# A routed-expert loop on one Trainium2 core: the down products moved one expert later, half of their weights split into two rounded parts, and five buffers for high parts instead of four

## The reference, cut to what matters

```python
def moe(hn, router_w, router_b, w_gu, b_gu, w_down, b_down):
    ...
    top_vals, top_idx = lax.top_k(logits, TOP_K)
    gates = jax.nn.softmax(top_vals, axis=-1)
    ...
    gu = lax.ragged_dot(xs, w_gu, group_sizes) + b_gu[sorted_e]
    gate = jnp.minimum(gu[:, ::2], SWIGLU_LIMIT)
    up = jnp.clip(gu[:, 1::2], -SWIGLU_LIMIT, SWIGLU_LIMIT)
    act = (up + 1.0) * (gate * jax.nn.sigmoid(SWIGLU_ALPHA * gate))
    y = lax.ragged_dot(act.astype(w_down.dtype), w_down, group_sizes) + b_down[sorted_e]
    y = y * gates.reshape(-1)[order][:, None].astype(y.dtype)
    out = jnp.zeros_like(xt).at[tok].add(y.astype(xt.dtype))
```

## Time and profile before

| | |
|---|---|
| three runs, median (range) | 3121.55 us (3121.18 to 3123.78) |
| span of the profiled execution | 3126.7 us |
| what lies around its span | no row gives it; span less median is 5.15 us |
| experts, from the start of the second to the end of the last | 422.60 to 1688.10 us, 31 experts |
| PE busy | 2762.4 us, 88% of the span |
| DVE, ACT, POOL busy | 56%, 37%, 9% |
| DMA, mean over the span | 203 GB/s |

### The profile page before, as it was taken

How to read it: one execution, slowest core, us unless ns; L and a number is a source line. 1 busy time by engine, 2 the same in 40 slices (tenths; PEclk the granted TensorE clock), 3 DMA queues, 4 the chain that set the end, 5 groups by cost and what they waited for, 6 DMA issues and landing times.

```text
span 3126.7 us, 32895 instructions
## 1 busy us (share of the span) xinstructions
PE 2762.4 (88%) x11604; PEld 2039.8 (65%) x11604; DVE 1756.8 (56%) x1942; ACT 1170.9 (37%) x1248; POOL 279.3 (9%) x336
## 2 busy tenths in 40 slices
PE   6987589999999999999996673498999989799997
PEld 4766456666666666666664343476888868588885
DVE  5764646666555555666664973546763354443333
ACT  4232345555555555555552130233222232232321
POOL 1230310000000000000002900000110000000000
PEclk9998699999999999999998785798999999999998
DMA  6742579999999999999996109333774333223432
GB/s 238 251 112 102 178 283 334 335 341 335 336 334 330 333 331 330 335 332 337 335 338 220 40 0 100 46 100 116 221 211 109 92 94 81 67 81 94 112 93 64
DMA packets 368731, 634.93 MB, mean 203 GB/s; under 512 B 45020, under 2 KB 238756, under 8 KB 368484
## 3 DMA queue, kind: packets, MB, share of 16 engines
q1 hardware_dynamic: 346244, 539.29, 54.0%
q0 software_dynamic: 17296, 76.03, 7.2%
q10 hardware_dynamic: 5136, 18.88, 1.5%
HBM read 610.10 MB, written 24.58 MB: 203 GB/s over the span
## 4 chain that ended last, share of the span: by engine, by line
PE 79%; DVE 10%; DMA 4%; ACT 2%; SPq 2%; POOL 1%; issue 1%; DVEq 0%; POOLq 0%; ACTq 0%
PE bank L1933 22%; PE bank L1949 15%; PE bank L2094 10%; PE bank L2095 10%; PE bank L2100 10%; PE bank L1922 2%; SPq L480 2%; PE bank L1911 1%; PE bank L1917 1%; PE bank L1760 1%; DMA ring<-k_dram 1%; PE bank L1795 1%; DVE work L1497 1%; PE bank L1796 1%; PE bank L1797 1%
## 5 line engine op out<-in xcount | busy, mean ns | idle before, releaser
L1415 DVE TENSOR_TENSOR gu_lo<-ring,gu_hi_ca 128x2048 fp32r<-128x2048 f32 x128 | 290.7, 2292 | 461.4 <-ACT gu_hi_ca L870 461.2
L1949 PE MATMUL bank<-ring,work 128*128 128x512 f32 x1024 | 458.9, 601 | 22.0 <-ACT work L882 22.0
L1949 PEld LDWEIGHTS bank<-ring,work 128*128 128x128 f32 x1024 | 190.2, 191 | 257.3 <-issue 227.7
L1933 PE MATMUL bank<-gu_lo,xs_hi 128*128 128x512 f32 x1024 | 316.1, 390 | 0.0
L1415 DVE TENSOR_TENSOR gu_lo<-ring,gu_hi_nat 128x2048 fp32r<-128x2048 f32 x128 | 290.7, 2291 | 28.8 <-ACT gu_hi_nat L870 28.3
L2094 PE MATMUL bank<-h_hi,fin_hi 128*128 128x512 f32 x704 | 277.7, 395 | 22.1 <-ACT h_hi L972 22.1
L2095 PE MATMUL bank<-h_hi,fin_lo 128*128 128x512 f32 x704 | 276.4, 393 | 0.0
L870 ACT ACTIVATE gu_hi_nat<-ring 128x2048 fp32r<-128x2048 f32 x128 | 241.9, 1920 | 51.1 <-PE bank L1933 51.1
L870 ACT ACTIVATE gu_hi_ca<-ring 128x2048 fp32r<-128x2048 f32 x128 | 241.5, 1910 | 42.6 <-PE bank L1933 39.0
L1933 PEld LDWEIGHTS bank<-gu_lo,xs_hi 128*128 128x128 f32 x1024 | 192.5, 188 | 40.5
L1013 ACT ACTIVATE fin_hi<-rows 128x1024 fp32r<-128x1024 f32 x88 | 88.2, 1052 | 213.5 <-DMA rows<-in_w_ffn_in 213.5
(11 more groups left out here) (425 smaller groups left out, 4521.3 us busy)
## 6 DMA issues: line engine op xcount, KB each, us to landing
...
ring<-in_expert_w_down SPq DMA_DIRECT2D x128, 1024.0 KB, 5.8
...
```

The source lines that it names most:

```text
L1415: tt(gu_lo[:, q], slot[q], whole(gu_hi[q % 4]), ALU.subtract).then_inc(s_gu_lo, 1)
L1933: last = mm(ps[2 * h + n][:], x[:, k, :], w[:, 512 * n:512 * (n + 1)], start=False, stop=(k == KD - 1 and w is lo))
L1949: last = mm(ps[4 + n][:], act_t[h][:, k, :], slot[q][:, k % 2, 512 * n:512 * (n + 1)], start=False, stop=(h == 1 and k == 3))
```

## The change

The expert loop is written anew as a pipeline, on all engines:

- The down products of expert e - 1 are made in the turn of expert e, behind its up products. All eight transposes of the activations stand together, between the first and second half of the up products of the next expert. Expert 0 has only up products; the last down products stand behind the loop.
- Of the four down slots, two (8 and 9, `SPLIT_DOWN = 2`) are split and made of three fp32r products, as the up slots are; for them the first half of the activations is split as well (`hidden_high`, `hidden_low`). Slots 10 and 11 stay plain float32 (`down_whole`).
- There are five buffers of high parts, `slot_hi`, and the split of a slot is issued four slots ahead (`LEAD`), when PE is through with the slot before the one it is at. Inside a slot PE now does all products with the high part first and then waits for the low part.
- A count of finished slots (`s_slot_done`) takes the place of three semaphores. SP loads the up slots of expert e + 1 and the down slots of expert e in the turn of e.
- The down bias leaves the loop. After the loop PE multiplies the gates, as a dense 32 x 512 matrix, with the down biases (8 products in float32, K = 32), and DVE adds the results to `rows` ahead of `combine`. For that DVE builds the dense gates behind the router's chain, and PE and ACT transpose and copy them.
- The activation is written with three DVE operations instead of six: the sigmoid reads the unclamped value from PSUM and is limited afterwards (`SIG_MAX`); the 1.0 that was added to `up` is added once to the bias rows, by POOL, ahead of their split.
- At the head of the loop ACT runs a sigmoid on one element.

The core of the diff:

```diff
--- before.py
+++ after.py
+HI_BUFS = 5
+SPLIT_DOWN = 2
+SPLIT = 8 + SPLIT_DOWN
+SIG_MAX = 1.0 / (1.0 + math.exp(-ALPHA * LIMIT))
+LEAD = HI_BUFS - 1
 LINEAR = ("glu", "fin0", "fout0", "cin", "cout", "fin1", "fout1")
...
+        def done_at(e, j):
+            return j if isinstance(e, int) and e == 0 else e * 12 + (j - 4)
+        def hi_of(e, j):
+            return slot_hi[(j if isinstance(e, int) and e == 0 else 8 + j) % HI_BUFS]
+        def ahead_of(e, j):
+            n = 8 if isinstance(e, int) and e == 0 else SPLIT
+            return (e, j + LEAD) if j + LEAD < n else (e + 1, j + LEAD - n)
+        def is_split(e, j):
+            return j < (SPLIT_DOWN if isinstance(e, int) and e == E else SPLIT)
...
-            def stream(tile, expert):
-                for q in range(12):
-
-                    if q in (3, 7):
-                        sp.wait_ge(s_gu_ready, 2 * tile - 1 + q // 4)
-                    elif q == 11:
-                        sp.wait_ge(s_y_ready, tile)
-                    else:
-                        sp.wait_ge(s_slot_free, 9 * tile - 8 + q - q // 4)
+            def load_up(tile, expert, used):
+                for q in range(8):
+                    sp.wait_ge(s_slot_done, used + q)
                     load_slot(q, expert)
+            def load_down(tile, expert, used):
+                for d in range(4):
+                    sp.wait_ge(s_slot_done, used + d)
+                    load_slot(8 + d, expert)
 
...
             for half in range(2):
-                pp = slice(E * half, E * (half + 1))
-                load(bias_rows[pp, 0:2 * D], a["expert_b_gate_up"][0], s_bias_in)
-                load(bias_rows[pp, 2 * D:], a["expert_b_down"][0], s_bias_in)
+                load(bias_rows[E * half:E * (half + 1), :], a["expert_b_gate_up"][0], s_bias_in)
+            load(down_bias, a["expert_b_down"][0], s_bias_in)
             for q in range(8, 12):
                 load_slot(q, 0)
-            with sp.Fori(1, E) as e:
-                stream(e, e)
+            load_up(1, 1, 1)
+            with sp.Fori(1, E - 1) as e:
+                load_up(e + 1, e + 1, e * 12 - 3)
+                load_down(e, e, e * 12 + 5)
+            load_down(E - 1, E - 1, 12 * (E - 1) + 5)
...
+            pool.wait_ge(s_bias_in, 48)
+            up_bias = bias_rows.rearrange("e (f two) -> e f two", two=2)[:, :, 1]
+            pool.tensor_scalar(up_bias, up_bias, 1.0, None, ALU.add).then_inc(s_bias_one, 1)
...
+            def split_high(e, j):
+                q = slot_of(e, j)
+                act.wait_ge(s_slot_in[q], e * 16 + (16 if q < 8 else 0))
+                back = j - HI_BUFS
+                if isinstance(e, int) and e <= 1:
+                    if e == 1 or back >= 0:
+                        act.wait_ge(s_slot_done, (done_at(e, back) if back >= 0 else 8 + back) + 1)
+                else:
+                    act.wait_ge(s_slot_done, (done_at(e, back) if back >= 0 else done_at(e - 1, SPLIT + back)) + 1)
+                act.activation(hi_of(e, j), slot[q], ACT.Copy).then_inc(s_slot_hi, 1)
+            def high_ahead(e, j):
+                if is_split(e, j) and is_split(*ahead_of(e, j)):
+                    split_high(*ahead_of(e, j))
...
+            def sigmoid(tile, h, done):
+                act.wait_ge(s_slot_done, done)
+                if not (isinstance(tile, int) and tile == 0):
+                    act.wait_ge(s_act_ready, tile * 2 + (h - 1))
+                act.activation(t_s[h], pairs[h][:].rearrange("p (f two) -> p f two", two=2)[:, :, 0],
+                               ACT.Sigmoid, scale=ALPHA).then_inc(s_sig_ready, 1)
+            def hidden_high(tile, h):
+                act.wait_ge(s_actt_ps, tile * 2 + (h + 1))
+                act.activation(act_f if h else act_hi[h], ps[6 + h].rearrange("p (k t) -> p k t", k=4), ACT.Copy).then_inc(s_actt_hi, 1)
...
+            def expert(e, stores, follows):
+                for j in range(12):
+                    high_ahead(e, j)
+                    if j == 1 and stores:
+                        store_y(e - 2, done_at(e - 1, 11) + 1, y_dram[bass.ds(e * P - 2 * P, P), :])
+                    if j == 4:
+                        hidden_high(e - 1, 0)
+                        hidden_high(e - 1, 1)
+                        sigmoid(e, 0, done_at(e, 3) + 1)
+                    if j == 8:
+                        tokens_columns(e + 1)
+                        sigmoid(e, 1, done_at(e, 7) + 1)
+                    if j == 9 and follows:
+                        pick_biases(e + 1)
...
+            for j in range(LEAD):
+                split_high(0, j)
+            act.wait_ge(s_gates_ps, 1)
+            act.activation(gates_t, ps[0][0:E, :], ACT.Copy).then_inc(s_prep_act, 1)
...
+            step(tt(prod, hot, gates.unsqueeze(3).broadcast_to([P, NT, TOPK, E]), ALU.mult))
+            dve.tensor_reduce(logits, prod.rearrange("p i k e -> p i e k"), AXX, ALU.add).then_inc(s_prep_dve, 1)
...
+                dve.wait_ge(s_sig_ready, tile * 2 + (h + 1))
+                if not (isinstance(tile, int) and tile == 0):
+                    dve.wait_ge(s_actt_ps, tile * 2 + (h - 1))
+                v = pairs[h][:].rearrange("p (f two) -> p f two", two=2)
+                step(ts(act_n[h], v[:, :, 1], LIMIT + 1.0, 1.0 - LIMIT, ALU.min, ALU.max))
+                step(stt(act_n[h], t_s[h], SIG_MAX, act_n[h], ALU.min, ALU.mult))
+                stt(act_n[h], v[:, :, 0], LIMIT, act_n[h], ALU.min, ALU.mult).then_inc(s_act_ready, 1)
...
+            def expert(e):
+                for j in range(12):
+                    low_ahead(e, j)
+                    if j == 1:
+                        swiglu(e - 1, 1)
+                    if j == 5:
+                        hidden_low(e - 1)
+                    if j == 7:
+                        swiglu(e, 0)
+                    if j == 9:
+                        tokens_low(e + 1)
...
+            for i in range(NT):
+                dve.wait_ge(s_gates_ps, i + 2)
+                tt(rows[:, i, :], rows[:, i, :], pairs[i][:], ALU.add).then_inc(s_prep_dve, 1)
...
+            def hidden_columns(tile):
+                for h in range(2):
+                    pe.wait_ge(s_act_ready, tile * 2 + (h + 1))
+                    for k in range(4):
+                        last = pe.transpose(ps[6 + h][:, P * k:P * (k + 1)], act_n[h][:, P * k:P * (k + 1)], ident)
...
+            def matmuls(banks, lhs, hi, lo, begins, ends, ready):
+                for lower in range(2):
+                    if lower:
+                        pe.wait_ge(s_slot_lo, ready)
+                    else:
+                        pe.wait_ge(s_slot_hi, ready)
+                    for k in range(2):
+                        for x in ((lhs[0],) if lower else lhs):
+                            for n in range(2):
+                                last = mm(ps[banks + n], x[:, k, :], (lo if lower else hi)[:, k, 512 * n:512 * (n + 1)],
+                                          start=(begins and lower == 0 and k == 0 and x is lhs[0]),
+                                          stop=(ends and lower == 1 and k == 1))
+                last.then_inc(s_slot_done, 1)
...
+            def down_whole(d, tile):
+                pe.wait_ge(s_slot_in[8 + d], tile * 16 + 16)
+                for k in range(2):
                     for n in range(2):
...
+                        last = mm(ps[4 + n], act_f[:, 2 * (d % 2) + k, :], slot[8 + d][:, k, 512 * n:512 * (n + 1)],
+                                  start=False, stop=(d == 3 and k == 1))
...
+            def expert(e):
+                pe.wait_ge(s_pick, e + 1)
+                pe.wait_ge(s_xst_ready, e * 2 + 2)
+                pe.wait_ge(s_act_ready, e * 2 - 1)
+                biases(0)
+                for j in range(4):
+                    up(j, hi_of(e, j), split_at(e, j) + 1)
+                hidden_columns(e - 1)
+                biases(1)
+                for j in range(4, 8):
+                    up(j, hi_of(e, j), split_at(e, j) + 1)
+                hidden_taken(e - 1)
+                tokens_columns(e + 1)
+                pe.wait_ge(s_y_sb, e * 2 - 1)
+                for j in range(8, SPLIT):
+                    down(j - 8, hi_of(e, j), split_at(e, j) + 1)
+                for d in range(SPLIT_DOWN, 4):
+                    down_whole(d, e - 1)
...
+            pe.wait_ge(s_prep_dve, 2)
+            for i in range(NT):
+                last = pe.transpose(ps[0][0:E, P * i:P * (i + 1)], route[:, E * i:E * (i + 1)], ident)
+            last.then_inc(s_gates_ps, 1)
             tokens_columns(0)
-            pe.wait_ge(s_bias_ok, 1)
-            with pe.Fori(0, E) as e:
+            pe.wait_ge(s_prep_dve, 1)
+            pe.wait_ge(s_prep_act, 2)
+            pe.wait_ge(s_xst_ready, 2)
+            for j in range(8):
+                if j % 4 == 0:
+                    biases(j // 4)
+                up(j, hi_of(0, j), j + 1)
+            tokens_columns(1)
+            with pe.Fori(1, E) as e:
```

(8 more changed lines are left out.)

315 lines of the change are left out of this document (151 added, 164 removed).

## The result

The changed kernel takes 3045.67 us (median of 4 runs, 3037.04 to 3049.77), the kernel before 3121.36 us (median of 4 runs, 3120.61 to 3123.78): a ratio of 0.9753, 95% interval 0.9737 to 0.9769. The forecast was 3036, with a range of 3022 to 3060. The profiled execution took 3049.77 us, its span is 3048.1 us. By spans 78.6 us were saved, where the prediction has 85.9.

A forecast was written before the change was run, and what follows sets the result against it. PE's own work was taken as the bound. PE ending the experts 88.6 us earlier, less 2.7 behind the loop, gave 85.9: 3126.7 to 3040.8, and a median 5.15 below the span, 3035.6 (3036); range 3022 to 3060.

The forecast's parts named there:

- PE bounds the turn: Expert loop: PE's products set each expert's turn, 37.75 us against 40.82 before; the likeliest case, chance 0.72.
- 2.3 for the clock: Start of expert 1: PE's lowered clock after its pause was to add 2.3 us.
- Two down slots to three products, 1.57: Expert turn on PE: two float32 down slots at 6.97 us become split slots at 5.40, saving 1.57.
- The rest of the change: Expert turn on PE: the other edits, such as moved transposes and down biases out of the loop, were to save 1.5 us.
- Waits inside a slot, nothing: Expert loop on PE: 22 waits an expert instead of 12 cost 0; rival 0.05 us each, chance 0.08.
- DMA is no bound: Expert loop: the bytes need 35.2 us of the 37.75 us turn; the rival that DMA bounds it had chance 0.13.
- The latest link: Expert turn: DVE's second-half activation of the expert before is ready 1.7 us before PE's transposes, the thinnest cover.
- (a): Before expert 1: POOL's added bias-row operation, with less ACT and DVE work, nets +1 us, between -2 and +2.
- (b): Before expert 1: extra DVE splits slow POOL's power table between first and second gather, +5 us, between 0 and +7.
- (d): After the last turn: copies 3.2 us, then the last down products at 5.40 and 7.07, 15.7 in all.
- Behind the loop: After the last store: eight float32 bias products on PE delay the first `combine` by 2.7 us, between 0 and 5.

## Why the prediction was right, and where it missed

**PE bounds the turn: right.** The turn without DMA, ACT or DVE in its way was forecast as 37.75 and is 37.63. PE never waits in the loop; the kernel with half the products shows that the other links can do 33.07, and the ones with no or four splits move by PE's products alone, 39.02 and 36.21. By the windows the 31 turns gave 96.3 us (1265.50 - 1169.16), where 95.2 less 2.3 for the clock were forecast, 3.4 better. The clock cost what was forecast: 1169.16 is 2.6 over 31 x 37.63.

**Two down slots to three products, 1.57: a little less.** It was 1.39 and 1.42 us by two experiments. The sum took two float32 slots away at the 6.97 of the earlier trace rows; but four in a row are 13.94 and the two that stay behind split slots are 7.18, so only 6.76 went, against 5.34 for the two split ones. The rest of the change gave more than forecast, 1.82 for 1.5: the second biases take 0.66 where the sum kept 0.97, four float32 slots in a row 13.94 for 14.04, and the sixteen transposes 2.19 for 2.02.

**Waits inside a slot, nothing: right,** 0.0015 us each at most. **DMA is no bound: right,** with a floor (35.2) that was set 2 us too high.

**The latest link: right.** DVE's activation of the second half ends at 915.49 (914.80 + 0.69, timeline of DVE), and its transposes begin at 916.93: 1.4 us of cover for a forecast of 1.7. Even with four splits it held.

**(a) and (b), the start: (b) right, (a) with the wrong sign.** From the first to the second gather of tokens it is 43.57 us (37.08 before), +6.5, where (b) has +5 with a range of 0 to 7. POOL's operations stand there at 0.32 or at 2.25 us, as in the earlier trace rows. With three splits made ahead instead of four the same stretch is 41.6 in both kernels that have it, so each split of DVE ahead of the tokens costs POOL's table about 2 us. That a DVE operation with both inputs in SBUF keeps a POOL operation that reads SBUF off a shared port for its whole length is what the Trainium skill says (SBUF — State Buffer, SBUF: two separate sides), and 2.25 beside 2.29 us agrees with it. The first gather itself stands 353.3 to 362.3 over twelve executions, against 358.93 before, but that spread lies ahead of (a): DVE's first row of the router's chain (L1387, behind PE's router products) starts between 315.80 and 324.77, with 324.77 in the first profile, 319.13 in its repeat and 319.07 before. From there to the first gather it is 36.8 to 38.3 us over the twelve, 37.50 in the first profile, and 39.86 before. So (a), forecast as +1 between -2 and +2, is -2.4. Of this 1.6 is a term that the prediction does not have: POOL's index operation ahead of the gather takes 0.51 us (361.59), where before it ran beside a DVE split and took 2.11 (356.65). Expert 1 begins at 413.8 instead of 411.2, 2.6 late: 5.7 are the late start of the router's chain, which is chance, -3.4 are (a), 1.5 are (b), and -1.2 the shorter way from the second gather to expert 1 (7.93 us for 9.17).

**(d), the tail: the step that failed.** It has "3.2, with DVE's low part beside the last copy; then 5.40 + 7.07: 15.7", and the tail took 24.2, 8.5 more. The step counted what ACT does from the end of the last turn on, and took the last activation as done by then. It left out that in the last turn the splits of the down slots stand ahead of the last sigmoid on ACT and ahead of the last expert's activation on DVE, and that those slots are freed only in this same turn, so that a DMA stands in between. With the splits put behind on both engines, 17.4 are measured: 3.2 for the copies, 7.2 for the two split slots, of which 1.8 are the low clock behind PE's pause (0.76 over the 7.2), and 7.0. So 6.8 of the 8.5 are shown to be the place of these splits, and the 1.8 of the clock is a term that was missing.

**Behind the loop.** The products were to cost 2.7, between 0 and 5, and cost 4.4 (14.98 - 10.59): the bound at half clock, 13.9, was the measure (14.02). Putting four of them ahead gives 5.7 back. Not in the prediction at all is the landing of the last store: 5.5 us for 3.1 before, in a repeat of the same kernel 3.1 too, and 7.4 to 7.9 in four kernels with a shorter tail. The store comes the nearer to the next stage's loads, which SP issues from the end of the last turn on, the shorter the tail is, and it lands the later for it (table above). With the tail of the changed kernel 5.5 came in one of five executions, and 3.1 to 3.2 in the other four; with the shorter tail the store is late in all four.

**The sum.** By spans it is 3048.1 for the 3040.8 forecast: -3.4 for the turns, +2.6 for the start (of which 5.7 are chance), +8.5 for the tail, +2.4 for the store, +1.7 for the products and -4.5 in unchanged stages behind them, which vary by more than this. The median lies 9.7 above the forecast of 3036: these 7.3, and 2.7 more since it lies 2.4 below the span of the profiled execution, where the prediction took 5.15 over from one execution of the kernel before. That the whole came so near is in part luck, as the tail's 8.5 was met by 7.9 of the other sign.
